# Inverse square roots as exp(-0.5 ln x) on ScalarE instead of a square root on ScalarE and a reciprocal on VectorE, in an encoder block on one core

## What is computed

```python
h  = x
hn = rms_norm(h, norm_mix);  proj = hn @ w_in            # 2048 x 5248
y_r = rwkv7_bidirectional(shifted columns)               # 16 heads of 64, both directions
y_a = rms_norm(window_attention(q, k, v), att_out_gain)
h  = h + concat(y_r, y_a) @ w_out
h  = h + memory_cross_attention(rms_norm(h), rms_norm(mem))
h  = h + hierarchical_moe(rms_norm(h))                   # 32 experts of 2048 x 512
return rms_norm(h, final_norm)

rms_norm(x, g) = x * rsqrt(mean(x*x) + 1e-6) * g
```

## Time and profile before

| | |
|---|---|
| Time, median of 3 runs | 2156.12 us (2152.45 to 2157.86) |
| The profiled execution, own time | 2150.49 us, of which the span of the profile is 2148.3 us |
| PE busy | 1884.5 us (88%) |
| DVE busy | 529.0 us (25%), 1260 instructions |
| ACT busy | 402.8 us (19%), 1109 instructions |
| PE's clock, mean granted | 0.953 of full speed |
| HBM traffic | 498.8 MB read, 18.9 MB written |

### The profile page before, as it was taken

One profiled execution on the slowest core, in us unless ns is written; L12 is line 12 of the kernel. 1 busy time (PEld: TensorE's weight loads), 2 busy tenths in 40 slices (PEclk: granted clock), 3 DMA queues, 4 the chain that ended last, 5 costly groups with the idle time before them and its releaser, 6 DMA issues.

```text
span 2148.3 us, 29196 instructions
## 1 busy us (share of the span) xinstructions
PE 1884.5 (88%) x11710; PEld 1357.9 (63%) x11710; DVE 529.0 (25%) x1260; ACT 402.8 (19%) x1109; POOL 55.2 (3%) x95
## 2 busy tenths in 40 slices
PE   4899999789999999999987988888898998888883
PEld 3788887568888888446746655554555555555551
DVE  1011101777777775101132000000000000000002
ACT  2300001544444444001221000000000000000001
POOL 0000000000000000000000000000000000000000
PEclk9999999889999999999986999999999999999996
DMA  8424823000000002645321999999999999999993
GB/s 279 157 79 156 148 89 138 1 1 1 0 0 0 0 0 79 235 156 196 137 105 79 388 430 433 429 429 429 420 431 425 427 421 425 428 429 428 420 429 162
DMA packets 93162, 505.81 MB, mean 235 GB/s; under 512 B 39077, under 2 KB 43417, under 8 KB 74681
## 3 DMA queue, kind: packets, MB, share of 16 engines
q1 hardware_dynamic: 85456, 487.62, 56.0%
q0 software_dynamic: 6656, 14.12, 1.8%
q10 hardware_dynamic: 1000, 3.37, 0.5%
HBM read 498.76 MB, written 18.91 MB: 241 GB/s over the span
## 4 chain that ended last, share of the span: by engine, by line
PE 66%; DMA 24%; DVE 5%; ACT 2%; issue 2%; SPq 1%; DVEq 0%; ACTq 0%; POOLq 0%
DMA ring<-in_wu 23%; PE ps L1560 14%; PE ps L1221 13%; PE ps L1457 5%; PE ps L1379 3%; PE ps L1398 3%; PE ps L1599 3%; PE ps L1550 3%; PE ps L1475 3%; PE ps L1355 1%; PE ps L1404 1%; PE ps L1356 1%; PE ps L1516 1%; PE ps L1484 1%; SPq L264 1%
## 5 line engine op out<-in xcount | busy, mean ns | idle before, releaser
L1560 PE MATMUL ps<-ring,rkv 128*64 128x256 f32 x4096 | 480.5, 395 | 64.7 <-DMA ring<-in_wu 36.7
L1560 PEld LDWEIGHTS ps<-ring,rkv 128*64 128x64 f32 x4096 | 328.2, 143 | 226.3 <-DMA ring<-in_wu 47.1
L1221 PE MATMUL ps<-hnT,ring 128*128 128x256 f32 (+1 forms) x1280 | 279.1, 380 | 6.4 <-ACT gg L456 2.2
L1221 PEld LDWEIGHTS ps<-hnT,ring 128*128 128x128 f32 (+1 forms) x1280 | 238.8, 187 | 46.9 <-issue 8.7
L1599 PE MATMUL ps<-ring,gg 128*64 128x512 f32 x1024 | 238.4, 620 | 29.3 <-DMA ring<-in_wd 19.2
L1599 PEld LDWEIGHTS ps<-ring,gg 128*64 128x64 f32 x1024 | 83.8, 142 | 161.9 <-issue 139.5
L1167 DVE SCALAR_TENSOR_TENSOR gg<-ps,tmp,gg 128x256 f32<-128x256 f32 x32 | 15.5, 484 | 518.4 <-PE ps L1560 518.4
L1550 PE MATMUL ps<-hnT,sw 128*128 (+1 forms) x1024 | 121.0, 280 | 7.4 <-DVE hnT L1151 7.4
L1550 PEld LDWEIGHTS ps<-hnT,sw 128*128 128x128 f32 x1024 | 117.9, 195 | 13.3 <-issue 13.3
L1379 PE MATMUL ps<-ring 128*128 128x128 f32 x768 | 114.6, 275 | 0.0
L1379 PEld LDWEIGHTS ps<-ring 128*128 128x128 f32 x768 | 100.2, 192 | 0.6 <-ACT ring L547 0.2
(11 more groups left out here) (318 smaller groups left out, 1840.9 us busy)
## 6 DMA issues: line engine op xcount, KB each, us to landing
ring<-in_wg SPq DMA_DIRECT2D x32, 4096.0 KB, 20.0
ring<-in_wu SPq DMA_DIRECT2D x32, 4096.0 KB
ring<-in_wd SPq DMA_DIRECT2D x32, 4096.0 KB, 18.0
ring<-in_w_in SPq DMA_DIRECT2D x7, 4096.0 KB, 14.3
ring<-in_w_out SPq DMA_DIRECT2D x4, 4096.0 KB, 19.6
ring<-in_w_in SPq DMA_DIRECT2D x16, 512.0 KB, 7.5
ring<-in_xatt_wk SPq DMA_DIRECT2D x1, 4096.0 KB, 15.1
ring<-in_xatt_wv SPq DMA_DIRECT2D x1, 4096.0 KB, 13.6
```

Source lines behind the costliest of these rows:

```text
L1221: ins = mm(ps[0:rows_, t % 4, 0:T], lhs, hnT[:, k, :], start=k == 0, stop=k == KD - 1)
L1560: ins = mm(ps[CAP * h:CAP * h + CAP, bank, 0:T], xT[:, k, CAP * i:CAP * i + CAP], slot_k(slot)[:, k, T * h:T * h + T], start=k == 0, stop= ...
```

## The change

A helper on ACT issues two instructions, a natural logarithm and an exponential with scale -0.5, with a wait for the first one's end between them. It takes the place of each of the square roots, and each reciprocal on DVE that followed one is left out. DVE's waits stay, and the count of chained instructions of one pass of its loop falls from 58 to 56. ACT's loop over pairs 1 to 6 now counts its chain.

```diff
+            def inverse_root(dst, src):
+                ac.link(A(dst, src, ACT.Ln))
+                return A(dst, dst, ACT.Exp, scale=-0.5)
...
             def std(n, turn_):
                 act.wait_ge(S["var_done"], turn_)
-                A(stat(n, 2), stat(n, 1), ACT.Sqrt).then_inc(S["std_done"], 1)
+                inverse_root(stat(n, 2), stat(n, 1)).then_inc(S["std_done"], 1)
...
             def key_norm(p):
                 act.wait_ge(S["rw_n2e"], p + 1)
-                A(ew[:, SQ], ew[:, SQ], ACT.Sqrt).then_inc(S["rw_nrm"], 1)
+                inverse_root(ew[:, SQ], ew[:, SQ]).then_inc(S["rw_nrm"], 1)
 
             def head_std(p):
                 act.wait_ge(S["rw_vare"], p + 1)
-                A(VAR, VAR, ACT.Sqrt).then_inc(S["rw_std"], 1)
+                inverse_root(VAR, VAR).then_inc(S["rw_std"], 1)
...
             with act.Fori(0, CT - 2) as i:
+                ac.enter(i, 2)
                 pair_(i + 1, False, False)
+                ac.leave(2, CT - 2)
...
-                A(stat(3, 2)[:, b:b + 1], stat(3, 1)[:, b:b + 1], ACT.Sqrt).then_inc(S["std_done"], 1)
+                inverse_root(stat(3, 2)[:, b:b + 1], stat(3, 1)[:, b:b + 1]).then_inc(S["std_done"], 1)
...
-                A(stat(5, 2)[:, b:b + 1], stat(5, 1)[:, b:b + 1], ACT.Sqrt).then_inc(S["std_done"], 1)
+                inverse_root(stat(5, 2)[:, b:b + 1], stat(5, 1)[:, b:b + 1]).then_inc(S["std_done"], 1)
...
                 dve.wait_ge(S["std_done"], turn_)
-                dc.link(V.reciprocal(stat(n, 2), stat(n, 2)))
...
                 dve.wait_ge(S["std_done"], turn_)
-                dc.link(V.reciprocal(stat(n, 2)[:, one], stat(n, 2)[:, one]))
...
             def key_norms(p):
                 dve.wait_ge(S["rw_nrm"], p + 1)
-                dc.add(V.reciprocal(ew[:, SQ], ew[:, SQ]))
...
             def inverse_std(p):
                 dve.wait_ge(S["rw_std"], p + 1)
-                dc.add(V.reciprocal(VAR, VAR))
...
-            PER = 58
+            PER = 56
```

## The result

| | before | after |
|---|---|---|
| Time, median | 2154.4 us (4 runs) | 2192.3 us (2191.6 to 2193.1, 4 runs) |
| Ratio | | 1.0174, 95% interval 1.0157 to 1.0192 |
| Span of the profile | 2148.3 us | 2189.6 us |
| ACT busy | 402.8 us | 444.1 us |
| DVE busy | 529.0 us | 504.4 us |

The change costs 37.9 us (34 to 41 us by the interval); 39.5 us and a time of 2196 us were forecast. The spans of the two profiles differ by 41.3 us. Some of that is not the change: in the profile after the input projection, which is the same code, had a mean clock of 0.94 between 110 and 140 us (1.00 before), and norm 4's mean, where the first inverse root in the chain begins, comes at 426.8 us instead of 425.1. In the eleven profiles of this case that mean comes between 424.8 and 430.2 us, in no order by old or new form, so single executions already differ by some us before the stages compared here.

The account below looks back on a forecast made before the run. PE was taken to bound the chain, waiting on ACT's loads. Terms 28.6 - 3.2 + 2.4 - 0.3 + 2.6 + 2.6 + 6.8 = 39.5 us on 2156.1 gave 2196 us, range 2184 to 2207.

Parts of the forecast that it names:

- rival 2: Whole kernel: two loads for each inverse root, but PE's clock never falls at the new wait; 2189 us, chance 0.2.
- Rival 3: Whole kernel: two loads, each new wait costing PE more than one slow stretch, +12 to 20 us; 2202 to 2209 us, chance 0.15.
- Two loads for each inverse root: Every inverse root on ACT: Ln and Exp each load their own table, 1.29 us a load; bounds 0 and 2 loads.
- Rival 1: Whole kernel: one table serves Ln and Exp, so the change is not slower; 2151 us, down to 2146, chance 0.08.
- ACT's stretch in level 1: Pairs 1 to 6, first load to level 2's first copy: 6.74 us after the change, against 1.92 before.
- PE has 0.05 us in hand: PE's level 2 transposes, pairs 1 to 6: only 0.05 us of ACT's 4.82 us delay absorbed; 4.77 us idle a pair.
- Level 5: Exponentials in seven pairs: the table load in front goes, gaining 0.45 us each, -3.2 us; other bound 1.28 us each, -9.0.
- The clock: PE's clock in the pairs: a fall in four of six, 1.7 us each, +6.8 us; bounds 0 and 20 us.
- Pair 0 and pair 7: Level 1 of the outer pairs, one root each: one load and one root more, 1.2 us each, +2.4 us for both.
- Set-up: Norm 4 and key norms before the pairs: added loads against the reciprocal removed, net -0.3 us, between -1.75 and +1.5.
- Norms 3 and 5: Norm 3 and the final norm: Exp's load is new in the chain for both blocks, +2.6 us for each norm.
- No cost for norms 1 and 2 and the last pair's root: Those three places: the new form adds nothing, as ACT idles 101.8, 13.7 and 9.06 us there.

## Why the prediction was right

The time, 2192.3 us, lies in the range of 2184 to 2207, 3.7 us below the forecast; 1.8 us of these are the median of the kernel before, which has settled that much lower. The time alone would not part the forecast from rival 2 (2189 us, no fall behind the wait); the clock in the windows and the kernel with PE kept busy do. Rival 3 fell too: the clock cost 8 us, not 12 to 20. That the pairs came out at 34.2 us, with 34.6 forecast, is partly luck: the clock cost 1.5 us more than its term, and the wait and level 5 together 2 us less. By the steps:

- **Two loads for each inverse root: right.** 24 and 24 loads. Rival 1 fell for this program as built, and was the right account of the other program: with the table chosen by hand, the kernel took 11.1 us less than the one before, where 5 to 10 us less had been worked out, without the 1.3 us of a final load done in advance. In that run one table serves both functions, with 7 loads in the whole program; where the builder chose, it was 53. A load costs hardly more than its own length: the row behind a load of 1.28 us starts 0.01 to 0.02 us later in the timelines above, and two loads more took PE's wait from 0.69 to 3.26 us, 1.29 us each.
- **ACT's stretch in level 1: right.** 6.80 us against 6.74.
- **PE has 0.05 us in hand: mis-sized.** Without a fall of the clock the new wait costs 56.03 - 51.44 = 4.6 us a pair, not 4.77; with both logarithms first it is 53.18 - 51.44 = 1.74 us for 2.04 us of longer stretch; with one load more 0.93 us for 1.30. There were about 0.3 us in hand, not 0.05. The step that failed took the merged row of four copies, 1.44 us, as the time that four copies need. Cut apart, the fourth copy of the kernel before starts late:

```profile
569.03 0.38 ACT L552 ACTIVATE ring<-ps 128x256 f32<-128x256 f32 x1
...
569.82 0.38 ACT L552 ACTIVATE ring<-ps 128x256 f32<-128x256 f32 x1
```

The first three follow each other by 0.27 us, the fourth waits for PE's last power matmul, which ends at 569.78 us. So ACT could have come 0.2 to 0.3 us later at no cost; the four copies alone take 1.19 us, as the profile after shows. Six pairs: 1.0 us.
- **Level 5: right, slightly low.** 0.61 us a pair (51.44 against 52.05, the kernel with the joint table), 0.45 forecast. The bound of 1.28 was far off, for the reason given: DVE is late next.
- **The clock: right in kind, the count and the price wrong in opposite ways.** Four falls in six pairs were the author's estimate. The fall came behind all six waits, not four, at 1.5 us each and not 1.7: 9 us, and pair 1, with a fall twice as long and a mean clock of 0.92, took 1 us more. At level 5 the profile after has two falls instead of three, 1.7 us back. Together 8.3 us, 6.8 forecast. The kernel with PE kept busy has shown that PE's idleness in this wait brings it: with PE idle for 4.24 to 4.28 us all six pairs had the fall, with matmuls in the wait none of them (1.00 over 3.4 us).
- **Pair 0 and pair 7: right.** +0.6 us for pair 0 (1.2 less the gain at level 5 was forecast, 0.75) and +1.2 us for pair 7.
- **Set-up: right.** -0.25 us, -0.3 forecast; the reciprocal's 1.75 us came off and the loads put it back.
- **Norms 3 and 5: right in the trace,** +2.6 and +2.8 us against 2.6 each; in the timed runs of the norms alone they came out smaller, as told above.
- **No cost for norms 1 and 2 and the last pair's root: right;** the stage that holds them takes 246.8 us in both profiles. For norm 0 it is consistent with the sum, but was not tried by itself. DVE's waits at steps 11 and 13 never reached PE, even where one grew to 3.36 us.
- **Small slips in the working, without effect on the forecast:** 2188.8 us and six falls of 1.7 us give 2199 as the forecast's upper end, not 2201; 12 us above the sum without falls gives 2201 for rival 3, not 2202; and the range's lower end comes to 2183, not 2184.

## What to carry to other kernels

Count the table loads before counting functions: a cheaper formula on ACT that alternates between two functions can cost two loads each time (here 48 loads of 1.28 us for 24 roots), and whether one table serves both depends on who chooses it (53 loads in the program by the builder, 7 with three asked for by hand), so look for loads in the profile and ask for the joint table by hand. Ask of the engine that feeds the bounding one how late it may come at each place; two loads and four functions cost 1.7 us a pair in one level and nothing when spread over two levels. Cut merged rows apart before taking slack from them, and price a long wait of PE with the slow stretch behind it (1.5 us a pair here, behind 4.2 to 4.3 us).

## What the runs showed that was not expected

The falls of the clock at level 5 (0.50 to 0.54 of full speed over 3.4 us in every profile that has them) are not explained. All these kernels leave PE little used there for about the same time (0.6 us less where the exponentials have no load), with a last wait of 1.22 us, yet the profiles have falls at level 5 in three of seven pairs before, two after, three with both logarithms first, one with two levels, none with the joint table, in every middle pair with one load more, and in two or three in the others. At 1.7 us each they move the time of such a profile by up to 10 us, more than the added load itself cost in that last experiment (5.6 us). So 5 us of the joint table's gain of 11 rest on falls that did not come, and whether they stay away in every execution wasn't tried.

In front of the transposes of level 2 the clock stayed up behind waits of 0.69 and 1.43 us (six each, 1.00 of full speed over the 3.4 us from the start of the transposes) and fell at every one of 3.3 us (six, 0.54 to 0.69) and of 4.2 to 4.3 us (six in the changed kernel, 0.50 to 0.64, and six with the pairs alone, 0.51 to 0.64).
